# Output projection by seven half-size products, and the order of work where the mixer begins

## The reference

```
z = h @ w_mix_in                      # columns: q, k, v, g_lr, og, cu (2 x 1024), gates (2 x 1024)
u = ua * sigmoid(ub); u = causal_depthwise_conv(u, 31 taps) ...
y_conv = u @ conv_w_proj
m = (gate_a * y_gla + gate_b * y_conv) @ w_mix_out      # 1024 x 1024 @ 1024 x 1024
x = x + rms_norm(m, mix_post_g)
f = swiglu_ffn(rms_norm(x, ffn2_pre_g), ...)
```

## Time and profile before

| | us |
|---|---|
| median of 3 runs (lowest, highest) | 2284.16 (2284.09, 2287.57) |
| the profiled execution's own time | 2283.87 |
| its span, first to last instruction | 2282.0 |
| mean granted TensorE clock, share of full | 0.998 |

### The profile page before, as it was taken

One profiled execution on the slowest core, in us unless ns is written; L12 is line 12 of the kernel. 1 busy time (PEld: TensorE's weight loads), 2 busy tenths in 40 slices (PEclk: granted clock), 3 DMA queues, 4 the chain that ended last, 5 costly groups with the idle time before them and its releaser, 6 DMA issues.

```text
span 2282.0 us, 29796 instructions
## 1 busy us (share of the span) xinstructions
PE 2257.2 (99%) x10620; PEld 1873.9 (82%) x10620; DVE 1586.8 (70%) x1916; ACT 880.2 (39%) x1321; POOL 907.4 (40%) x641
## 2 busy tenths in 40 slices
PE   8999999999998999999999999999999999999998
PEld 5888888888886888898998987888888888888887
DVE  8866666677878877698787828542686666658677
ACT  5433333343564343344344432412443333334443
POOL 3455555200438877612122154224464545440002
PEclk9999999999999999999999999999999999999999
DMA  5333333466842343321121143535232424238576
GB/s 158 112 96 110 97 109 98 170 190 209 274 150 74 93 139 102 127 78 57 56 68 45 47 166 139 183 112 175 84 92 86 120 86 121 85 102 266 159 222 231
DMA packets 235284, 290.28 MB, mean 127 GB/s; under 512 B 11568, under 2 KB 160816, under 8 KB 232368
## 3 DMA queue, kind: packets, MB, share of 16 engines
q1 hardware_dynamic: 232464, 283.71, 39.2%
q10 hardware_dynamic: 2720, 5.24, 0.6%
HBM read 212.36 MB, written 76.55 MB: 127 GB/s over the span
## 4 chain that ended last, share of the span: by engine, by line
PE 67%; DVE 1%; POOL 1%; issue 1%; ACT 0%; DMA 0%; POOLq 0%; DVEq 0%; ACTq 0%
PE PU L930 7%; PE PU L932 6%; PE PU L931 6%; PE PU L1106 4%; PE PU L1107 4%; PE PU L1105 4%; PE PU L1010 4%; PE PU L1012 3%; PE PU L1011 3%; PE PU L1256 2%; PE PU L1257 2%; PE PU L1258 2%; PE PG L1106 2%; PE PG L1107 2%; PE PG L1105 2%; PE PG L1348 1%
## 5 line engine op out<-in xcount | busy, mean ns | idle before, releaser
L3122 POOL TENSOR_TENSOR ws<-pw,ws 128x512 fp32r<-128x512 f32 x168 | 243.7, 1454 | 215.5 <-ACT ws L1622 185.4
L930 PE MATMUL PU<-XH,w_h 128*128 128x512 f32 x576 | 229.2, 398 | 0.5 <-issue 0.5
L3122 POOL TENSOR_TENSOR ws<-s_sum,ws 128x512 fp32r<-128x512 f32 x122 | 159.6, 1317 | 174.0 <-ACT ws L1622 174.0
L932 PE MATMUL PU<-XH,w_l 128*128 128x512 f32 x576 | 224.6, 390 | 0.0
L931 PE MATMUL PU<-XL,w_h 128*128 128x512 f32 x576 | 224.2, 389 | 0.0
L3202 POOL TENSOR_SCALAR st<-st 128x1 f32<-128x1 f32 (+1 forms) x40 | 16.9, 423 | 477.8 <-ACT junk L1558 195.2
L2448 DVE TENSOR_TENSOR f_l<-f_raw,f_h 128x1024 fp32r<-128x1024 f32 x110 | 139.4, 1272 | 57.7 <-ACT f_h L1801 57.6
L1801 ACT ACTIVATE f_h<-f_raw 128x1024 fp32r<-128x1024 f32 x110 | 116.5, 1060 | 144.2 <-PE PG L1258 54.9
L1622 ACT ACTIVATE ws<-s_sum 128x512 fp32r<-128x512 f32 x123 | 75.3, 630 | 246.1 <-DVE s_sum L2302 141.4
L1622 ACT ACTIVATE ws<-pw 128x512 fp32r<-128x512 f32 x172 | 107.1, 628 | 153.6 <-PE PU L1107 150.2
L2324 DVE TENSOR_TENSOR u<-PU,u 128x512 f32<-128x512 f32 x80 | 55.3, 691 | 148.0 <-PE PU L1107 148.0
(11 more groups left out here) (503 smaller groups left out, 6345.2 us busy)
## 6 DMA issues: line engine op xcount, KB each, us to landing
pw<-in_ffn_w_in SPq DMA_DIRECT2D x86, 512.0 KB, 5.8
f_raw<-f_d SPq DMA_DIRECT2D x154, 256.0 KB, 3.1
f_raw<-in_ffn_w_out SPq DMA_DIRECT2D x132, 256.0 KB, 4.3
w_raw<-in_w_mix_in SPq DMA_DIRECT2D x56, 512.0 KB, 4.8
f_d<-s_buf SPq DMA_DIRECT2D x22, 1024.0 KB, 5.0
f_d<-hid SPq DMA_DIRECT2D x21, 512.0 KB, 2.6
x_d<-FACC SPq DMA_DIRECT2D x16, 512.0 KB, 3.2
gate_d<-tmp SPq DMA_DIRECT2D x14, 512.0 KB, 3.4
```

The costliest lines, as they stand in the source:

```text
L930: pe.matmul(dst, hi(k), xh(k), start=(n == 0), stop=False)
L932: last = pe.matmul(dst, lo(k), xh(k), start=False, stop=(n == KT - 1))
L3122: PT(ws[:, i, 1, :, :], form_source(name, par), ws[:, i, 0, :, :], ALU.subtract).then_inc(form_lo, 1)
```

## The change

**Output projection.** `HW`, `o_raw`, `o_h`, `o_l`, `hf` go. `HR` holds the unsplit hidden tiles, `WQ` the four 512x512 quarters of the weight (four DMAs in place of eight). Seven products in the order P1, P7, P6, P5, P4, P3, P2, each of four steps m (l = 4 x product + m, 28 steps; 4 token tiles x 3 matmuls per step), so 7 x 4 x 4 blocks of three matmuls. The hidden side's sums S1 to S4 (16 of 128x512) are POOL's (`hidden_sum`), the weight side's T3 (one 128x2048) and T2, T1, T4 (12 of 128x512) DVE's (`weight_sum`). For each step ACT makes two hi parts (`out_hi`), DVE the hidden lo (`out_lo`), POOL the weight lo (`out_lo`), all 128x512, into nine sets of buffers; for most steps the hi part waits until PE has finished the step four before. Each of the seven results is drained by DVE, four banks a product, 36 instructions of 128x512 in all in place of 16. Tiles 0 to 3 are whole after P4, tiles 4 to 7 after P2, the last product. The norm's order follows: on DVE `post` of tile 0 stands after the drains of P4, the drains of P3 and P2 around `pre(2), pre(3)`, and `post` and `pre` of tiles 4 to 7 behind the last product. `POOL_TILES` becomes (5, 7) for this norm.

**Mixer entry.** DVE's `rank_lo(1)` moves behind the third `t_step`. POOL's first `u_gate` moves ahead of the four `mix_rest(0, ...)`. In `period(0)` POOL's three sums of pair 1 move behind the lo parts of A11(1), A22(0), A12(1), S4(0). ACT's copy of P7(0) moves ahead of the forms S2(1), S1(1).

```diff
@@ names
+M_ORDER = ("P1", "P7", "P6", "P5", "P4", "P3", "P2")
+M_CONV = (*range(11), 24, 11, 12, 13, 26, 14, 15, 16, 25, *range(17, 24), 27)
+POOL_TILES = ((1, 3), (5, 7), (1, 3))
@@ PE
+                for l in range(N_M):
+                    q, m = l // 4, l % 4
+                    banks, tail = (MB, XB)[q % 2], M_TAIL.get(M_ORDER[q], 1)
+                    if 4 - tail <= m < 3:
+                        continue
+                    if m < 3:
+                        ready(l)
+                    for t in range(4):
+                        if m == 0:
+                            bank_free(q, t)
+                        if m < 3:
+                            last = block(banks[t], m_set(l), t, m == 0, False)
+                            continue
+                        for x in range(l - tail + 1, l + 1):
+                            if t == 0:
+                                ready(x)
+                            last = block(banks[t], m_set(x), t, False, x == l)
+                        last.then_inc(y_done, 1)
@@ ACT
+                elif l == 25:
+                    act.wait_ge(mh_lo, nth(15))
...
+                elif l > 5 and m == 3:
+                    act.wait_ge(y_done, 4 * (l // 4 - 1) + 4)
+                elif l > 5:
+                    act.wait_ge(m_step, M_STEP_0 + 3 * (l // 4 - 1) + m + 1)
+                A(m_h[s][:, 0, :], m_hidden(l), ACT.Copy)
+                A(m_h[s][:, 1, :], m_weights(l), ACT.Copy).then_inc(m_hi, 1)
...
+            for l in M_CONV[:nth(25)]:
+                out_hi(l)
+            act.wait_ge(mw_lo, nth(15))
+            front_forms(1, 0, 3)
+            out_hi(17)
+            front_forms(1, 3, 6)
+            for l in range(18, 24):
+                out_hi(l)
@@ DVE
+                TT_(m_l[s][:, 0, :], m_hidden(l), m_h[s][:, 0, :], ALU.subtract).then_inc(mh_lo, 1)
...
+            out_lo(2), out_lo(3)
+            for l in M_CONV[nth(3):nth(23)]:
+                out_lo(l)
+                if 4 <= l < 8:
+                    weight_sum("T2", l - 4), weight_sum("T1", l - 4)
+                elif 11 <= l < 15:
+                    weight_sum("T4", l - 11)
+                if l in (6, 10, 14, 18, 22):
+                    for t in range(4):
+                        mix_drain(M_ORDER[(l - 6) // 4], t)
+            post(0, 1), out_lo(27), post(1, 1), pre(0), post(2, 1), pre(1), post(3, 1)
             for t in range(4):
+                mix_drain("P3", t)
+            pre(2), pre(3)
+            for t in range(4):
+                mix_drain("P2", t)
             x_rest(1, "B11")
+            post(4, 1)
             x_rest(1, "B21")
+            post(5, 1), post(6, 1), pre(4), post(7, 1), pre(5), pre(6), pre(7)
@@ DVE, mixer entry
-            rank_lo(1)
             dve.wait_ge(t_step, T_STEP_0 + 1)
             TT_(t0[:, :, :], t0[:, :, :], quadrant(XL, "B12"), ALU.add).then_inc(t_step, 1)
+            rank_lo(1)
@@ POOL, mixer entry
+            u_gate(0)
+            for name in ("A11", "A12", "S2", "S1"):
+                mix_rest(0, name)
@@ POOL, output projection
+                PT(m_l[s][:, 1, :], m_weights(l), m_h[s][:, 1, :], ALU.subtract).then_inc(mw_lo, 1)
...
+            for m in range(4):
+                hidden_sum("S3", m)
+            hidden_sum("S1", 0), hidden_sum("S1", 1), out_lo(0), out_lo(1), hidden_sum("S1", 2), hidden_sum("S1", 3)
+            out_lo(2), out_lo(3)
+            for m in range(4):
+                out_lo(4 + m), hidden_sum("S2", m)
+            out_lo(8), hidden_sum("S4", 0), out_lo(9), hidden_sum("S4", 1), out_lo(10), hidden_sum("S4", 2), out_lo(24)
+            out_lo(11), hidden_sum("S4", 3)
+            for l in M_CONV[nth(11):nth(25)]:
+                out_lo(l)
+            front_forms(1, 0, 3), out_lo(17), front_forms(1, 3, 6), out_lo(18)
```

More of the change, by code:

```diff
@@ L546, in build @@
         second_full = [sem("second_full0"), sem("second_full1")]
+        m_step, wt_sum = scaled, c_sum
+        quarter_full = {"B11": (o_full[0], 16), "B12": (o_full[1], 16), "B22": (second_full[0], 32),
+                        "B21": (second_full[1], 32)}
         gt_full = [sem("gt_full0"), sem("gt_full1")]
@@ L886, in _ @@
                     sp.wait_ge(sq_sum, KT - 1)
-                    oraw(0)
-                    oraw(1)
+                    out_quarter("B11")
                 elif i < 3:
                     wide(s, s % 2, wcv, (i + 1) * 2 * P)
-            oraw(2)
+                    out_quarter("B12" if i == 1 else "B22")
+            out_quarter("B21")
             sp.wait_ge(mm_t, 7)
@@ L1032, in mix_out, with block, bank_free, ready @@
-            def mix_out():
[L1034 to L1054, removed]
+            def mix_out():
+                def block(dst, s, t, first, final):
+                    tok = slice(t * P, (t + 1) * P)
+                    pe.matmul(dst, m_h[s][:, 0, tok], m_h[s][:, 1, :], start=first, stop=False)
+                    pe.matmul(dst, m_h[s][:, 0, tok], m_l[s][:, 1, :], start=False, stop=False)
+                    return pe.matmul(dst, m_l[s][:, 0, tok], m_h[s][:, 1, :], start=False, stop=final)
+                def bank_free(q, t):
+                    if q == 0:
+                        g_wait(t // 2, G_CP // 2)
+                    elif q == 1:
+                        pe.wait_ge(unit_free[t // 2], U_END // 2)
+                    else:
+                        pe.wait_ge(y_drained, m_drained(M_ORDER[q - 2], t))
+                def ready(l):
+                    pe.wait_ge(mh_lo, nth(l))
+                    pe.wait_ge(mw_lo, nth(l))
+                for l in range(N_M):
[16 more added lines that the diff above has]
+                        last.then_inc(y_done, 1)
+                    if m < 3:
+                        last.then_inc(m_step, 1)
@@ new lines, in weight_sum @@
+            def weight_sum(name, m):
+                b11, t3, b21, b22 = (WQ[f][:, m, :] for f in ("B11", "B12", "B21", "B22"))
+                t1, t2 = (WT[:, x, m, :] for x in range(2))
+                dst, x, y, op = {"T2": (t2, t3, b11, ALU.add), "T1": (t1, b22, t2, ALU.subtract),
+                                 "T4": (fourth(m), b21, t2, ALU.subtract)}[name]
+                if name == "T2":
+                    dve.wait_ge(unit_done, U_END)
+                    dve.wait_ge(wt_sum, W_SUM_0 + 1)
+                elif name == "T1":
+                    dve.wait_ge(wt_sum, W_SUM_0 + t_made("T2", m))
+                else:
+                    dve.wait_ge(*quarter_full["B21"])
+                    dve.wait_ge(mw_lo, nth(8 + m))
+                    dve.wait_ge(wt_sum, W_SUM_0 + t_made("T1", m))
+                TT_(dst, x, y, op).then_inc(wt_sum, 1)
@@ L3073, in _ @@
                     gated(3, 1)
+            dve.wait_ge(ct_lo, 2 * KT)
             for i in range(4):
+                if i == 3:
+                    out_lo(0), out_lo(1)
+                    for form in ("B12", "B22", "B11"):
+                        dve.wait_ge(*quarter_full[form])
+                    TT_(WQ["B12"][:, :, :], WQ["B22"][:, :, :], WQ["B12"][:, :, :], ALU.subtract).then_inc(wt_sum, 1)
                 for half in range(2):
@@ L3329, in _ @@
                 .then_inc(w_lo, 1)
-            for name in ("A11", "A12", "S2", "S1"):
-                mix_rest(0, name)
             pool.wait_ge(rank_hi, 3)
```

243 lines of the change are left out of this document (141 added, 102 removed).

## The result

The changed kernel takes 2300.03 us (median of 4 runs, 2299.37 to 2300.88), the kernel before in the same session 2284.12 (2282.90 to 2287.57): ratio 1.0067, interval [1.0054, 1.0079]. The forecast was 2294.6, in a range of 2284 to 2303: slower for the reason given, but by 15.9 us and not by 10.5. The profiled executions have spans of 2299.1 and 2282.0: 17.1 to find.

What follows compares the result with a forecast made beforehand. PE, busy 99% of the span, bounds the kernel, so only fewer matmuls or changed waits matter. 2283.87 - 3.2 (entry) + 13.7 (exit) = 2294.4, or 2294.6 for the runs' median; range 2284 to 2303.

Steps and rivals of the forecast that it cites:

- The direction: Whole kernel: the change makes it slower, chance 0.78, against 0.07 for the same and 0.15 for faster.
- the exit: Output projection up to B12: matmuls saved, stalls and the waits at B11 and B21 sum to +13.7 us.
- The price, 1.70 per pair as 0.60 + 1.10: Projection: a DVE instruction with two SBUF inputs and one of POOL run in turn, 1.70 us per pair.
- Matmuls removed, -10.9: Output projection: 336 matmuls in place of 384, 48 x 0.2267 = 10.9 us less.
- the stalls, 8.0 and 9.9: Projection: PE waits for DVE's and POOL's parts, 8.0 us at steps 6 to 8, 9.9 at steps 15 to 18.
- Third stall, 4.9 before B11 and 1.8 at B21: After the projection: DVE's post, pre and drains delay B11 by 4.9 us; ACT's later B11 fill delays B21 by 1.8.
- After B12, nothing: What follows B12 is unchanged and begins with the same distances: no gain or loss.
- Entry, -3.2: Mixer entry: P5(1) starts at 745.4 instead of 748.67, 3.2 us gained, 4.7 of idle PE in place of 6.0.
- faster, turns don't matter: Rival, projection: 128x512 instructions are not held by turns, the matmuls' gain stays, 2275.8 us; chance 0.15.
- half of the stalls: Rival, exit: POOL or DVE catches up, only the first stall and B11's stay, 2284.8 to 2288; chance 0.12.
- Entry gains all: Rival, mixer entry: the taps don't hold P5(1), which starts at 740.7, 4.7 us more gained, 2289.9; chance 0.05.
- The clock: Rival, entry, steps 7, 15, 17, B11: waits bring PE's half clock, 1.86 us per case, 2298.3 to 2302; chance 0.2.

Runs made afterwards that it cites:

- experiments 4 and 5: Changed kernel with DVE's hidden lo parts as one-input instructions (2295.65; 2286.30), POOL's 16 sums as memsets (2296.21), or 13 weight lo parts moved to DVE (2295.92).
- one_input: Changed kernel with DVE's 28 hidden lo subtractions replaced by a tensor_scalar with one source in SBUF, timing only: 2295.65 us, ratio 1.0047 to the kernel before.
- proj_alone: Changed kernel with the mixer's entry of before, so only the output projection's change stays: 2298.75 us, ratio 1.0059 to the kernel before.
- entry_alone: Kernel before with only the changed mixer entry: 2283.92 us, ratio 0.9997 [0.9988, 1.0006] to the kernel before.
- taps_spread: Kernel before with the changed entry, two convolution taps instead of ten before C11(1)'s sum and four taps moved into the next four periods: 2278.24 us, ratio 0.9969.
- lo_on_dve: Changed kernel with POOL's 13 weight lo parts of steps 4 to 16 made by DVE: 2295.92 us, ratio 1.0047 to the kernel before.
- all_orders: Changed kernel with lo_on_dve, taps_spread's entry, and ACT's and POOL's six front forms one by one behind steps 17 to 22: 2285.82 us, ratio 1.0005.
- t1_later: Changed kernel with DVE's four T1 sums behind the lo parts of steps 8 to 11 instead of 4 to 7: 2299.02 us, ratio 1.0065.

## Why the prediction was right or wrong

The direction and the exit were right; the entry was wrong. In the profiles the exit lost 14.42 (7.03 + 5.59 + 1.80) against 13.7 forecast, the entry lost 0.55 where 3.2 were to be gained, and the LayerNorm's 1.99 was in no step.

- **The price, 1.70 per pair as 0.60 + 1.10:** right in size, and shown by experiments 4 and 5. In the rule's wording one half failed. Two SBUF inputs are not the only mark of a DVE instruction that is held: `one_input` has one and was held. The Trainium skill (SBUF — State Buffer, "Who interferes with whom") also counts DVE's two-port modes, which a tensor_scalar can enter, and says that a DVE instruction with two SBUF inputs does not contend with a GpSimd one that only writes. The traces agree with both: 1.51 for the tensor_scalar, 0.67 for the reduction, and a subtraction that goes on beside a memset. That `one_input`'s instruction ran in such a mode is inferred from its 0.45 from start to start.
- **Matmuls removed, -10.9, and the stalls, 8.0 and 9.9:** right; measured 7.73 and 9.92, a length of 94.07 for 94.0. Inside, it was less exact: step 16 was late by 2.56, at the half clock, and step 17 by 1.12 in place of 3.4. POOL's lo(17) came when it was forecast, and the slow matmuls lay ahead of it, in time that PE would have waited anyway. The same holds for step 7's slow matmuls and step 8. `proj_alone` is the control: there step 8 was as late (2.36) with no slow matmul in step 7, and steps 16 and 17 were late by 0.13 and 3.52 in place of 2.56 and 1.12, the same sum. So a clock drop ahead of another stall cost nothing, and the rival that charged 1.86 for each priced the wrong thing here.
- **Third stall, 4.9 before B11 and 1.8 at B21:** measured 5.44 and 1.80 (3.90 from B11 to B21 against 2.10). Both are right in kind. The 1.8 is ACT's order, as forecast: its fill came 1.82 later behind B11's first transpose (2.46 against 0.64), and from the fill's start to B21 it took 1.44 against 1.46. The transposes themselves ran at the half clock behind the wait, 2.82 for twelve where the earlier trace rows have 1.47, but in time in which B21 would have waited for the fill; its own wait was left at 0.45. This is read from the trace, and the same in all nine profiles with the new projection; no run moves ACT's sums.
- **After B12, nothing:** 0.1.
- **Entry, -3.2:** this is the step that failed. P5(1) was to start at 745.4 and did at 746.26: the pads were set 0.4 later than forecast, the load of `ub` took 0.2 more, and the pass from the sum to the matmul was not counted. The rest is the clock. The forecast called the 1.86 of a slow P1(1) gone with its wait, and wrote in the same paragraph that 4.7 of idle PE stay at P5(1), without charging any price there; it left that to a rival. The price was 2.96, and the entry lost 0.55 in the profile and gained nothing beyond `entry_alone`'s interval. Before the runs one case stood for this price, the 5.97 of the earlier trace rows. Now there are twelve: behind each wait of 4.2 to 6.0 us that stands before 128x512 matmuls in these stages of the fourteen profiles, matmuls 0.43 apart follow, 5 to 13 distances of them (in one case after three at full rate).
- **The LayerNorm's 1.99:** in no step of the forecast. Of it 1.6 come and go with the execution; what share of that lies between the medians, no run here separates.
- **The rivals:** "faster, turns don't matter" and "half of the stalls" fell. "Entry gains all" fell for this order, but `taps_spread` shows that the reason given, ten taps ahead of one sum, was the right one. "The clock" happened, with one case that cost (the entry) and three that were covered (steps 7 and 15, B11). That the time fell near this rival's 2298.3 to 2302 is therefore partly luck.

## What to carry to other kernels

Strassen's products trade matmuls for additions and lo parts, and the trade pays only where the engines that make them have room: count DVE's and POOL's instructions not as two loads but as one, wherever POOL reads SBUF and DVE's instruction is of a kind that was held here (two SBUF inputs, or the tensor_scalar). Give an instruction that either can do to the engine that needs less of the common time for it, even if it is the busier one (0.60 on DVE against 1.10 on POOL), and ask what the next stage wants from that engine, since PE's earlier end is worth nothing if DVE's queue sets the next start. A wait that goes can uncover the next one. A long idle time of PE costs more than its length where no other wait follows (2.96 more in the entry), and the slow matmuls behind it are free where PE would wait again.

## What the runs showed of the hardware

- A DVE tensor_scalar with one source in SBUF, 0.45 us from start to start alone, took 1.51 beside POOL; a reduction over an axis of one element, 0.67 long alone, took 0.67 beside it. A POOL memset of 128x512 takes 0.52 and did not hold DVE's subtraction, which ended 0.55 after POOL's reading instruction did.
- After a wait of 2.56 us at step 5, the half clock showed in `lo_on_dve` (1556.98 to 1559.96) and not in `all_orders`, with the same wait in the same place. Of nine waits of 3.23 to 3.38 in the projection, the half clock showed at once behind five, after four full-rate matmuls behind two, and behind two (`proj_alone` at step 7, `t1_later` at step 17) only after the next wait. What decides, no run here shows.
- Sixteen one-column matmuls, 1.95 us in which PE counts as busy, were followed by the half clock in 8 of 14 profiles, at 1.6 us a time: from their start to the projection it is 111.34 to 111.40 us in these eight (111.37 after) and 109.67 to 109.78 in the other six (109.78 before).
